# Projection steps between attention units, head-by-head turning back, and the angle steps of a rotary table in a fused two-block kernel

## The chip, the cores and the metric

One NeuronCore of a Trainium2 chip runs the whole program. The metric is the device time of one execution in microseconds (us), and of several executions the median. PE is TensorE, DVE VectorE, ACT ScalarE, POOL GpSimd, SP SyncE, whose queue issues the weight loads.

## What is computed

Two transformer blocks on one sequence of 512 tokens of 1024 channels, all in fp32. Cut to what matters here:

```
# first block (16 meta tokens in front: 528 positions)
z = rms(h) @ w_in            -> q, k, v, glu, g_att, g_conv
o = differential attention of 8 heads, block-causal mask
y_att = rms(o per head) * sub_w * 0.8
u = glu gate -> causal depthwise convolution of 31 taps -> layernorm -> silu
h = h + (sigmoid(g_att) * y_att + sigmoid(g_conv) * (u @ w_conv_out)) @ w_out
h = h + (silu(gate) * val) @ w_down      # gate, val: 3-tap conv of rms(h) @ w_up
# second block, two layers
ang = positions * inv_freq;  cos(ang), sin(ang) rotate q and k
retention of 8 heads beside a gated 3-tap convolution, one output product
```

## The kernel before, in words

Every fp32 product runs as three fp32r passes. A block of weights, 1024 x 256 (1 MB), is loaded into one of two `raw` buffers by SP's queue. ACT rounds it into `w_hi` (L965), DVE subtracts to `w_lo` (L1390, `lo(j, b)`), and PE adds up lo x hi, hi x hi, hi x lo (L414, `tile`). A **step** is one slice k of 128 input channels for one of the two output halves: three passes of two 256-column pieces, six matmuls. SP loads block b+1 into a buffer only when the `w_lo` of block b is done. Order is written out by hand on each engine, with semaphores between them.

**Attention** (PE L533 on, DVE from L1526, ACT `heads` L1045). A loop of four passes, each over two heads. A pass has ten units (`UNITS`): for each head the meta rows and then four blocks of 128 query rows. For a unit PE makes the scores (L580 to L590), DVE masks them and takes the maximum (L1557 to L1568), ACT takes the exponentials, DVE combines the two maps of the differential attention (L1573 to L1581, semaphore `a_full`), PE turns the result (`turn`, L602 and L604), ACT copies it, PE multiplies with the values (`weigh`, L619 and L621), and ACT copies that and sums its squares. Between these parts PE runs `fill(n)`, the next n of 48 projection steps (`done`, numbers 0 to 47): steps 0 to 15 the gates of this pair, 16 to 31 the q of the next, 32 to 47 the k of the next, with `jj` 0 before `jj` 1. In the fourth pass the last 32 are two blocks of the convolution's gate. The value product (`v_block`, L548) stands at the head of each pass; its first part waits for the `w_lo` that DVE made at the end of the pass before (L1612). DVE fills its own waits with taps of the 31-tap convolution (`conv`, L1474).

At the end of a pass DVE squares the exponent sums, POOL takes a power (L348), DVE scales the meta rows of both heads (`o_meta`, L1603) and then the 512 rows of one head and of the other (`o_rows`, L1609), three signals of `o_scaled`. Then it makes `lo(0, b1 + 2)`. PE's `back` (L625 to L633) waits for all three signals and transposes both heads into PSUM; DVE multiplies them by the gate (L1618, L1619) into `oT`. POOL meanwhile adds the two finished channels of the convolution to `ssum` (L371).

Behind the fourth pass DVE makes one more `w_lo` (L1621, from a `w_hi` that ACT makes when step 47 is done), PE sums `ssum` over the channels (L675), which gives the mean of the layernorm (DVE L1624), runs two gate steps and broadcasts the mean (L682), and runs 15 more gate steps while DVE and ACT centre and square.

**Feed-forward** (PE `feed_forward` L703, DVE `up` L1699 and `add_to_h` L1671): the 22 channel groups come in three parts, g = 0, g = 1 and the last. Each ends in a residual: DVE adds the product to `h` (L1678). After g = 0 DVE converts the positions to float (L1738). After g = 1 PE spreads them over the partitions (L753, one row of fp32), DVE multiplies by the frequencies (L1750, `pos_done`) and reduces the angles to the range of the sine table, seven steps for the sine and seven for the cosine (L1753 to L1760), each waiting for the one before; PE waits for `pos_done` before the last part. ACT takes the sines much later.

Of the kernel before, what the change touches and what calls it, by code (L numbers as in the profile page):

```python
# [24 lines left out]
P = 128  # L25
D = 1024
KT = D // P
SEQ = 512
META = 16
# [25 lines left out]
PI_MAX = 3.1415925  # L55
# [4 lines left out]
B_GLU, B_ATT, B_CO, B_WO, B_FF, B_LAY = 0, 4, 14, 16, 18, 35  # L60
# [3 lines left out]
FF_B = 6  # L64
# [26 lines left out]
def build(nc, io, out):  # L91
# [14 lines left out]
    with ctx:  # L106
# [10 lines left out]
        h = sb("h", [P, KT, T1])  # L117
# [279 lines left out]
        def _(pe):  # L397
# [135 lines left out]
            with pe.Fori(0, 4) as i:  # L533
# [21 lines left out]
                def fill(n):  # L555

                    for x in range(done[0], done[0] + n):
                        c, jj, k = x // (2 * KT), x // KT % 2, x % KT
                        last = tile((1, 0, 1)[c], jj, f1 + 1 + c, b1 + (c + 1) // 2, n_hi, n_lo, T1 if c == 2 else T2,
                                    part=[k], c0=0 if c == 2 else OLD)  # L560
                        if k == KT - 1:
                            last.then_inc(acc_full[jj], 1)
                    done[0] += n
# [60 lines left out]

                def back():  # L625

                    pe.wait_ge(s["o_scaled"], i * 3 + 3)
                    pe.wait_ge(s["const_done"], 4)
                    for hh in range(2):
                        for q in range(NQT):  # L630
                            pe.transpose(sc[:, hh, q * P:(q + 1) * P], o_rows[:, hh, q * P:(q + 1) * P], ident[:, :])
                        last = pe.transpose(tr[:, 0, hh * META:(hh + 1) * META], o_meta[:, hh * P:(hh + 1) * P],
                                            ident[0:META, 0:META])  # L633
                    last.then_inc(s["o_turned"], 1)
# [10 lines left out]
                fill(2)  # L645
                weigh(0)

                for uu, (n0, n1) in enumerate(((2, 2), (2, 3), (5, 1), (1, 2), (1, 1), (2, 2), (2, 2), (4, 1)), 2):
                    scores(uu)
                    fill(n0)  # L650
                    turn(uu - 1)
                    fill(n1)
                    weigh(uu - 1)
                fill(1)
                turn(UNITS - 1)
                fill(2)
                weigh(UNITS - 1)
                fill(8)
                back()
                fill(2)  # L660
                assert done[0] == 3 * 2 * KT

            def g_conv(a, b):
# [39 lines left out]
            def feed_forward(b0, f0, g0, n, kt, first=False, last=False):  # L703
                y_hi, y_lo = (g_hi, g_lo) if last else (n_hi, n_lo)

                def up_pair(i, stats=False):
                    for x, (jj, ks) in enumerate(steps_in_turn(KT)):
                        step = tile(0, jj, i * 2 + f0, i + b0, m_hi, m_lo, T2, ready=None if jj else ("n_full", KT), part=ks, c0=C2)
                        if ks[-1] == KT - 1:
                            step.then_inc(acc_full[jj], 1)  # L710
                        if stats and x == 3:
                            pe.wait_ge(s["ss_full"], 2 * KT)
                            token_sums(ST_FFN, [ssum], T2 - P)
                        if stats and x == 9:
                            broadcast(ST_FFN, [tr], T2 - SEQ)
                    chunk(1, i + b0, i * 2 + f0 + 1, m_hi, m_lo, T2, c0=C2)

                if first:
                    up_pair(0, True)
                with pe.Fori(1 if first else 0, n) as i:  # L720
                    up_pair(i)
                b, f = b0 + n, f0 + 2 * n
                for j, ks in ((0, range(kt - 2)), (1, range(3)), (0, range(kt - 2, kt)), (1, range(3, kt))):
                    for jj in range(2):
                        step = tile(j, jj, f + j, b, y_hi, y_lo, SEQ, kt, ready=("gl_full", g0) if jj == 0 else None,
                                    part=ks, bank=j, e=f + j if j == 0 else f)
                        if ks[-1] == kt - 1:
                            step.then_inc(acc_full[jj], 1)
                for j in range(1 if last else 2):
                    for jj in range(2):  # L730
                        tile(j, jj, f + 2 + j, b + 1, y_hi, y_lo, SEQ, kt, bank=j,
                             e=f + 1 + j).then_inc(acc_full[jj], 1)
                if not last:
                    return

                pe.wait_ge(lo_full[1], b + 2)
                for c in range(2):
                    for jj in range(2):
                        if c == 0:
                            pe.wait_ge(evac[jj], f + 4)  # L740
                        for k in range(kt):
                            step = half_step(1, jj, c, k, y_hi, y_lo, start=k == 0, stop=k == kt - 1)
                            if (c, jj, k) == (1, 0, 4):
                                half_sums(0, 0)
                            if (c, jj, k) == (1, 1, 4):
                                half_broadcast(ST_LAY, 0)
                        step.then_inc(s["ha_full"] if c == 0 else acc_full[jj], 1)

            for g in range(2):
                feed_forward(g * FF_B + B_FF, g * (2 * FF_B) + 2 * B_FF, g * KT, 4, KT, g == 0)  # L750

            pe.wait_ge(s["pos_f"], 1)
            pe.matmul(sc[:, 0, 0:SEQ], ones[0:1, 0:1].to_broadcast([1, P]), sin[0:1, :], start=True,  # L753
                      stop=True).then_inc(s["pos_full"], 1)
            pe.wait_ge(s["pos_done"], 1)
            feed_forward(B_FF + 2 * FF_B, 2 * (B_FF + 2 * FF_B), 2 * KT, 3, FT - 2 * KT, last=True)

# [629 lines left out]
        def _(dve):  # L1387
# [138 lines left out]
            with dve.Fori(0, 4) as i:  # L1526
# [62 lines left out]
                for hh in range(2):  # L1589
# [10 lines left out]
                                         op1=ALU.add).then_inc(s["st_var"], 1)  # L1600
                conv(2 * A_TAPS - taps[0])
                dve.wait_ge(s["st_pow"], i + ST_HEADS + 1)
                dve.tensor_tensor(o_meta[:, 0:2 * P].rearrange("p (h n) -> p h n", n=P),  # L1603
                                  o_meta[:, 0:2 * P].rearrange("p (h n) -> p h n", n=P),
                                  pw[0:META, 8:10].rearrange("p (h o) -> p h o", o=1).to_broadcast([META, 2, P]),
                                  ALU.mult).then_inc(s["o_scaled"], 1)
                for hh in range(2):
                    rows_h = o_rows[:, hh, 0:SEQ].rearrange("p (q n) -> p q n", n=P)
                    dve.tensor_tensor(rows_h, rows_h,  # L1609
                                      pw[:, 4 * hh:4 * hh + 4].rearrange("p (q o) -> p q o", o=1).to_broadcast([P, NQT, P]),  # L1610
                                      ALU.mult).then_inc(s["o_scaled"], 1)
# [115 lines left out]
                                          ALU.subtract).then_inc(s["gl_full"], 1)  # L1727
                    dve.wait_ge(s["gl_full"], tl + 2)

            for g in range(2):  # L1730
                b_g = g * FF_B + B_FF
                f_g = g * (2 * FF_B) + 2 * B_FF
                up(b_g, f_g, g * KT, 4)
                for i in range(2):
                    add_to_h(i, b_g + i + 4, f_g + i * 2 + 8)
                if g == 0:
                    dve.wait_ge(s["ld_pos"], 16)
                    dve.tensor_copy(sin[0:1, :], cos[0:1, :].bitcast(i32)).then_inc(s["pos_f"], 1)  # L1738

            dve.wait_ge(s["pos_full"], 1)  # L1740
            ang, kk = decay[:, 0, :], decay[:, 1, :]
            trig = [0]

            def t_step(ins):
                trig[0] += 1
                ins.then_inc(s["trig"], 1)
                dve.wait_ge(s["trig"], trig[0])

            dve.wait_ge(s["ld_freq"], 16)
            dve.tensor_scalar(ang, sc[:, 0, :], freq[:, 0:1], None, ALU.mult).then_inc(s["pos_done"], 1)  # L1750
            dve.wait_ge(s["pos_done"], 1)
            for dst, turn in ((sin, 0.0), (cos, 0.25)):
                t_step(dve.tensor_scalar(kk, ang, 1.0 / TWO_PI, turn, ALU.mult, ALU.add))  # L1753
                t_step(dve.tensor_scalar(kk, kk, ROUND, ROUND, ALU.add, ALU.subtract))
                t_step(dve.scalar_tensor_tensor(out=dst[:, :], in0=kk, scalar=-PI_1, in1=ang, op0=ALU.mult, op1=ALU.add))
                for part in (PI_2, PI_3):
                    t_step(dve.scalar_tensor_tensor(out=dst[:, :], in0=kk, scalar=-part, in1=dst[:, :], op0=ALU.mult,
                                                    op1=ALU.add))
                t_step(dve.tensor_scalar(dst[:, :], dst[:, :], turn * TWO_PI, PI_MAX, ALU.add, ALU.min))
                last = dve.tensor_scalar(dst[:, :], dst[:, :], -PI_MAX, None, ALU.max)  # L1760
                if dst is sin:
                    t_step(last)
            last.then_inc(s["trig_s"], 1)

            up(B_FF + 2 * FF_B, 2 * (B_FF + 2 * FF_B), 2 * KT, 3, g_hi, g_lo)
            def lo_half(jj, l):
# [283 lines left out]
```

## Time and profile before

| | |
|---|---|
| median of 3 runs | 1924.81 us (1923.0 to 1926.1) |
| the profiled execution | 1927.68 us |
| its span, first to last instruction | 1925.9 us (1.8 us lie around it) |
| PE, DVE, ACT, POOL busy | 98%, 59%, 33%, 4% |
| mean granted TensorE clock | 0.993 of full speed |
| weight load of PE busy | 88% |

Busy shares say how full an engine is, not what it waits for; a granted clock of 1.00 is 2.4 GHz and 0.50 is 1.2 GHz. The four attention passes begin at 142.54, 214.31, 286.08 and 357.83 us. The boundary behind g = 0 is at about 694 us, the one behind g = 1 at about 829 us. The duration of a matmul in the rows overlaps its neighbours'.

### The profile page before, as it was taken

To read this page: it belongs to the slowest core of one execution; us is meant where nothing else is said; L and a number is where in the kernel's file an instruction comes from. 1 tells how busy PE (TensorE), PEld (TensorE's weight loads), DVE (VectorE), ACT (ScalarE), POOL (GpSimd) and SP (SyncE) were. 2 spreads that over 40 slices of the span, in tenths; PEclk is the share of its full clock that TensorE was granted. 3 is DMA by queue.
4 is the path that set the end of the run, shared out by engine and by line. 5 is a ranking of instruction groups with operands and counts; after the bars stand their busy time and mean duration, and the time that the engine had idled before them with its cause. 6 is when DMAs were issued, how large, how long until landed. Compare 5 with 4: busy or idle time off the path is not lost.

```text
span 1925.9 us, 30697 instructions
## 1 busy us (share of the span) xinstructions
PE 1895.4 (98%) x12195; PEld 1700.1 (88%) x12195; DVE 1127.3 (59%) x1554; ACT 634.2 (33%) x1105; POOL 70.0 (4%) x72
## 2 busy tenths in 40 slices
PE   7999999999999999999999999999999999999998
PEld 7998888889999999899988888888898888888888
DVE  5777887886556546566664554454256555544522
ACT  4224454445333323224522222222242222222222
POOL 1000110110000000000000000000000000000000
PEclk8999999999999999999999999999999999999999
DMA  5221211212232223322332323233222323232231
GB/s 160 87 88 45 70 57 53 73 53 67 89 100 96 87 88 99 97 88 66 99 99 66 98 76 109 87 91 106 89 73 91 99 77 97 88 107 89 88 108 44
DMA packets 159794, 165.89 MB, mean 86 GB/s; under 512 B 3032, under 2 KB 156129, under 8 KB 159730
## 3 DMA queue, kind: packets, MB, share of 16 engines
q1 hardware_dynamic: 156736, 160.51, 25.9%
q10 hardware_dynamic: 2674, 4.42, 0.7%
q8 instruction: 46, 0.75, 0.2%
q14 instruction: 18, 0.15, 0.0%
q0 software_dynamic: 320, 0.07, 0.0%
HBM read 162.88 MB, written 2.10 MB: 86 GB/s over the span
## 4 chain that ended last, share of the span: by engine, by line
PE 89%; DVE 5%; issue 4%; ACT 1%; DMA 0%; DVEq 0%; SPq 0%; ACTq 0%; POOLq 0%; POOL 0%
PE acc L414 70%; PE acc L809 4%; PE acc L548 3%; PE acc L480 2%; PE tr L845 2%; PE acc L773 1%; PE sc L831 1%; DVE y L1474 1%; PE sc L590 1%; DVE w_lo L1390 1%; PE tr L831 1%; PE tr L621 0%; DMA xs<-in_x 0%; PE tr L619 0%; PE sc L852 0%
## 5 line engine op out<-in xcount | busy, mean ns | idle before, releaser
L1390 DVE TENSOR_TENSOR w_lo<-raw,w_hi 128x2048 fp32r<-128x2048 f32 (+1 forms) x148 | 337.6, 2281 | 151.5 <-ACT w_hi L965 150.0
L965 ACT ACTIVATE w_hi<-raw 128x2048 fp32r<-128x2048 f32 x147 | 280.0, 1905 | 433.1 <-PE acc L414 426.6
L414 PE MATMUL acc<-s_lo,w_hi 128*128 128x512 f32 x848 | 333.0, 393 | 0.0
L414 PE MATMUL acc<-s_hi,w_lo 128*128 128x512 f32 x848 | 330.2, 389 | 0.0
L414 PE MATMUL acc<-s_hi,w_hi 128*128 128x512 f32 x848 | 330.1, 389 | 0.0
L414 PE MATMUL acc<-n_lo,w_hi 128*128 128x256 f32 (+3 forms) x1024 | 240.8, 306 | 4.4 <-DVE n_lo L1424 3.0
L414 PE MATMUL acc<-n_hi,w_hi 128*128 128x256 f32 (+3 forms) x1024 | 232.1, 298 | 0.0
L414 PE MATMUL acc<-n_hi,w_lo 128*128 128x256 f32 (+3 forms) x1024 | 231.7, 297 | 0.0
L414 PEld LDWEIGHTS acc<-s_hi,w_lo 128*128 128x128 f32 x848 | 159.2, 188 | 33.3
L414 PEld LDWEIGHTS acc<-s_lo,w_hi 128*128 128x128 f32 x848 | 159.3, 188 | 32.1
L414 PEld LDWEIGHTS acc<-s_hi,w_hi 128*128 128x128 f32 x848 | 159.3, 188 | 31.9
L414 PEld LDWEIGHTS acc<-n_lo,w_hi 128*128 128x128 f32 x1024 | 163.5, 190 | 25.0 <-issue 16.8
L414 PEld LDWEIGHTS acc<-n_hi,w_lo 128*128 128x128 f32 x1024 | 164.7, 190 | 5.1
L414 PEld LDWEIGHTS acc<-n_hi,w_hi 128*128 128x128 f32 x1024 | 164.6, 190 | 4.9
L414 PE MATMUL acc<-m_hi,w_hi 128*128 128x256 f32 x832 | 166.7, 281 | 0.0
L414 PE MATMUL acc<-m_hi,w_lo 128*128 128x256 f32 x832 | 166.2, 281 | 0.0
L1474 DVE SCALAR_TENSOR_TENSOR y<-u,par,y (+1 forms) x240 | 164.5, 747 | 1.7 <-DVE neg_lam L1523 0.4
L414 PE MATMUL acc<-m_lo,w_hi 128*128 128x256 f32 x704 | 142.1, 283 | 2.2 <-DVE decay L1750 1.2
L414 PEld LDWEIGHTS acc<-m_hi,w_hi 128*128 128x128 f32 x832 | 128.2, 189 | 0.0
L414 PEld LDWEIGHTS acc<-m_hi,w_lo 128*128 128x128 f32 x832 | 127.9, 189 | 0.0
L414 PEld LDWEIGHTS acc<-m_lo,w_hi 128*128 128x128 f32 x704 | 108.2, 189 | 5.1 <-DVE z L1707 2.3
L1883 DVE SCALAR_TENSOR_TENSOR st<-sc,pp,decay 128x512 f32<-128x512 f32 (+1 forms) x32 | 20.4, 680 | 96.3 <-PE tr L831 52.1
(305 smaller groups left out, 2877.7 us busy)
## 6 DMA issues: line engine op xcount, KB each, us to landing
raw<-in_w_in SPq DMA_DIRECT2D x92, 1024.0 KB, 5.3
raw<-in_w_up SPq DMA_DIRECT2D x22, 1024.0 KB, 5.1
raw<-in_w_out SPq DMA_DIRECT2D x20, 1024.0 KB, 5.1
raw<-in_w_down SPq DMA_DIRECT2D x8, 1024.0 KB, 5.0
raw<-in_w_conv_out SPq DMA_DIRECT2D x4, 1024.0 KB, 5.1
decay<-in_decay ACTq DMA_DIRECT2D x8, 512.0 KB, 5.2
raw<-in_w_down SPq DMA_DIRECT2D x4, 768.0 KB, 4.3
xs<-in_x SPq DMA_DIRECT2D x4, 512.0 KB, 5.8
```

The lines of the kernel that those rows point to most:

```text
L414: last = pe.matmul(acc[jj][:, bank, at_:at_ + n], w[j][:, k, jj * P:(jj + 1) * P], x[:, k0 + k, c:c + n], start=start and k == 0 and p == ...
L480: last = pe.matmul(acc[jj][:, c, cols], w[j][:, k, jj * P:(jj + 1) * P], x[:, k0 + k, cols], start=start and p == 0, stop=stop and p == 2)
L548: last = pe.matmul(dst, x[:, k, c:c + m], w[0][:, k, :], start=k == 0 and p == 0, stop=k == KT - 1 and p == 2)
L590: last = pe.matmul(sc[:, m, 0:keys], qs, kT[part, hh, 0:keys], start=True, stop=True)
L773: last = pe.matmul(acc[jj][:, j, cols], w[j][:, k, jj * P:(jj + 1) * P], x[:, k, cols], start=k == 0 and w is w_hi and x is s_hi, stop=k = ...
L809: last = pe.matmul(acc[jj][:, 0, (q % 2) * CW:(q % 2 + 1) * CW], x[:, k, q * P:(q + 1) * P], w[0][:, k, :], start=k == 0 and p == 0, stop= ...
L831: last = pe.matmul(dst, rk[:, hh, kb * P:(kb + 1) * P], rq[:, hh, kb * P:SEQ], start=True, stop=True)
L845: last = pe.matmul(dst[:, q * P:(q + 1) * P], st[:, c:c + P], rv[:, kb, hh * P:(hh + 1) * P], start=kb == 0, stop=kb == q)
L965: act.activation(w_hi[j][:, 0:kt, :], raw[j][:, 0:kt, :], ACT.Copy).then_inc(hi_full[j], 1)
L1390: dve.tensor_tensor(w_lo[j][:, 0:kt, :], raw[j][:, 0:kt, :], w_hi[j][:, 0:kt, :].bitcast(fp32), ALU.subtract).then_inc(lo_full[j], 1)
L1474: dve.scalar_tensor_tensor(out=dst, in0=src, scalar=w, in1=dst, op0=ALU.mult, op1=ALU.add).then_inc(s["conv"], 1)
L1883: last = dve.scalar_tensor_tensor(out=st[:, c:c + w], in0=src, scalar=pp2[:, kb:kb + 1], in1=decay[:, hh, 0:w], op0=ALU.mult, op1=ALU.mult)
```

## The change

Three things. **Placing of steps:** one more step before `weigh(7)` (`(2, 2)` to `(2, 3)`), one more before `turn(9)`, and the two steps behind `back` are gone; the total stays 48. **Turning back head by head:** DVE scales the rows of the first head first, then the meta rows, then the rows of the second; PE's `back` transposes the first head's rows after one signal, the second's after all three, and the meta rows last. **Angles:** the spread of the positions and the sine's steps move behind the residual of g = 0, the cosine's steps behind that of g = 1; the conversion of the positions moves ahead of the residual of g = 0. PE's wait for `pos_done` stays where it was.

```diff
                 def back():
 
-                    pe.wait_ge(s["o_scaled"], i * 3 + 3)
                     pe.wait_ge(s["const_done"], 4)
                     for hh in range(2):
+                        pe.wait_ge(s["o_scaled"], i * 3 + 2 * hh + 1)
                         for q in range(NQT):
                             pe.transpose(sc[:, hh, q * P:(q + 1) * P], o_rows[:, hh, q * P:(q + 1) * P], ident[:, :])
+                    for hh in range(2):
                         last = pe.transpose(tr[:, 0, hh * META:(hh + 1) * META], o_meta[:, hh * P:(hh + 1) * P],
                                             ident[0:META, 0:META])
...
-                for uu, (n0, n1) in enumerate(((2, 2), (2, 3), (5, 1), (1, 2), (1, 1), (2, 2), (2, 2), (4, 1)), 2):
+                for uu, (n0, n1) in enumerate(((2, 2), (2, 3), (5, 1), (1, 2), (1, 1), (2, 2), (2, 3), (4, 1)), 2):
                     scores(uu)
                     fill(n0)
                     turn(uu - 1)
                     fill(n1)
                     weigh(uu - 1)
-                fill(1)
+                fill(2)
                 turn(UNITS - 1)
                 fill(2)
                 weigh(UNITS - 1)
                 fill(8)
                 back()
-                fill(2)
...
             for g in range(2):
                 feed_forward(g * FF_B + B_FF, g * (2 * FF_B) + 2 * B_FF, g * KT, 4, KT, g == 0)
-
-            pe.wait_ge(s["pos_f"], 1)
-            pe.matmul(sc[:, 0, 0:SEQ], ones[0:1, 0:1].to_broadcast([1, P]), sin[0:1, :], start=True,
-                      stop=True).then_inc(s["pos_full"], 1)
+                if g == 0:
+                    pe.wait_ge(s["pos_f"], 1)
+                    pe.matmul(sc[:, 0, 0:SEQ], ones[0:1, 0:1].to_broadcast([1, P]), sin[0:1, :], start=True,
+                              stop=True).then_inc(s["pos_full"], 1)
+
             pe.wait_ge(s["pos_done"], 1)
...
+            for g in range(2):
...
+                up(b_g, f_g, g * KT, 4)
+                if g == 0:
+                    dve.wait_ge(s["ld_pos"], 16)
+                    dve.tensor_copy(sin[0:1, :], cos[0:1, :].bitcast(i32)).then_inc(s["pos_f"], 1)
+                for i in range(2):
+                    add_to_h(i, b_g + i + 4, f_g + i * 2 + 8)
+                if g == 0:
+                    dve.wait_ge(s["pos_full"], 1)
+                    dve.wait_ge(s["ld_freq"], 16)
+                    dve.tensor_scalar(ang, sc[:, 0, :], freq[:, 0:1], None, ALU.mult).then_inc(s["pos_done"], 1)
+                    dve.wait_ge(s["pos_done"], 1)
+                    t_step(angles(sin, 0.0))
+                else:
+                    angles(cos, 0.25).then_inc(s["trig_s"], 1)
```

The seven steps themselves are those of before, put into a function `angles(dst, turn)`. On DVE the three scaling products of L1603 and L1609 are the same, in the other order.

## Rows read from the trace of the kernel before

**Rows 1.** The page, busy time by engine

```profile
PE 1895.4 (98%) x12195; PEld 1700.1 (88%) x12195; DVE 1127.3 (59%) x1554; ACT 634.2 (33%) x1105; POOL 70.0 (4%) x72
```

**Rows 2.** Waits of the PE queue, whole run: engine line waited for: us, times, longest

```profile
PE tr L602 <- DVE e L1581: 2.0, 4, 0.5
...
PE sc L590 <- ACT e L1062: 1.4, 4, 0.4
...
PE sc L631 <- DVE rb L1609: 1.1, 4, 0.3
```

**Rows 3.** Timeline of PE, second pass over a head pair: start us, us, instruction

```profile
265.57 1.13 PE L590 MATMUL sc<-kT,qT 64*128 64x512 f32 x4 [0.36 <-ACT e L1062]
...
273.43 0.28 PE L602 MATMUL tr<-ident,e 128*16 128x128 f32 x1 [0.50 <-DVE e L1581]
...
282.87 0.65 PE L631 MATMUL sc<-ident,rb 128*128 128x128 f32 x4 [0.30 <-DVE rb L1609]
```

**Rows 4.** Chain that ended last, end of that pass: start us, us, what

```profile
284.43 1.65 PE acc L414 x12
...
286.08 2.72 PE acc L548 x24
```

**Rows 5.** Timeline of DVE, same pass

```profile
267.28 0.14 DVE L1557 MEMSET sc<- 64x96 f32 x1
...
271.90 0.16 DVE L1573 TENSOR_TENSOR eu<-eu 128x2 f32<-128x2 f32 x1
...
282.74 2.27 DVE L1390 TENSOR_TENSOR w_lo<-raw,w_hi 128x2048 fp32r<-128x2048 f32 x1
...
286.27 1.40 DVE L1474 SCALAR_TENSOR_TENSOR y<-u,par,y  x2
```

**Rows 6.** Timeline of POOL, same pass, and the end of the fourth

```profile
281.55 4.64 POOL L371 TENSOR_TENSOR ssum<-ssum,y 128x514 f32<-128x514 f32 x1 [0.39 <-DVE y L1474]
286.37 2.27 POOL L371 TENSOR_TENSOR ssum<-ssum,y 128x514 f32<-128x514 f32 x1 [0.18 <-POOL ssum L371]
...
429.86 1.10 POOL L371 TENSOR_TENSOR ssum<-ssum,y 128x514 f32<-128x514 f32 x1 [0.18 <-POOL ssum L371]
```

**Rows 7.** Timeline of PE behind the fourth pass

```profile
431.10 1.25 PE L675 MATMUL sc<-ones,ssum 128*128 128x1 f32 x10 [1.50 <-POOL ssum L371]
...
434.55 2.29 PE L682 MATMUL tr<-ident,var 128*128 128x128 f32 x10 [0.32 <-DVE var L1624]
```

**Rows 8.** Timeline of ACT behind the fourth pass

```profile
429.69 0.60 ACT L974 ACTIVATE ga<-acc 128x514 f32<-128x514 f32 x1 [6.61 <-PE acc L414]
430.19 1.90 ACT L965 ACTIVATE w_hi<-raw 128x2048 fp32r<-128x2048 f32 x1
```

**Rows 9.** Windows: stretch us, busy us by engine, PEclk, DMA share, GB/s

```profile
432.00:440.00 8.00, 7.68 (x41) 7.38 (x41) 5.20 (x7) 1.99 (x5) 0.00 (x0) 0.58 0.52 177
832.00:840.00 8.00, 8.00 (x57) 8.00 (x57) 7.62 (x13) 0.00 (x0) 0.00 (x0) 0.79 0.01 2
```

**Rows 10.** Chain that ended last, both group boundaries of the second feed-forward part

```profile
717.47 22.19 PE acc L414 x186
...
831.40 24.42 PE acc L414 x192
```

**Rows 11.** Timeline of PE at the second group boundary

```profile
829.06 1.12 PE L753 MATMUL sc<-sin,ones 1*128 1x512 f32 x2
831.40 0.47 PE L414 MATMUL acc<-m_lo,w_hi 128*128 128x256 f32 x2 [1.23 <-DVE decay L1750]
```

**Rows 12.** Timeline of DVE behind the first and the second group boundary

```profile
703.30 0.69 DVE L1707 TENSOR_TENSOR z<-acc,rb 128x514 f32<-128x514 f32 x1 [5.23 <-PE acc L414]
...
830.22 0.75 DVE L1750 TENSOR_SCALAR decay<-sc,freq 128x512 f32<-128x512 f32 x1 [0.36 <-PE sc L753]
...
838.93 2.28 DVE L1390 TENSOR_TENSOR w_lo<-raw,w_hi 128x2048 fp32r<-128x2048 f32 x1
```

**Rows 13.** The page, DMA issues: out<-in, queue, times, KB each, us to landing

```profile
raw<-in_w_up SPq DMA_DIRECT2D x22, 1024.0 KB, 5.1
```

More of the change, by code:

```diff
@@ L1602, in _ @@
                 dve.wait_ge(s["st_pow"], i + ST_HEADS + 1)
[L1603 to L1606, printed above, removed]
                 for hh in range(2):
+                    if hh == 1:
+                        dve.tensor_tensor(o_meta[:, 0:2 * P].rearrange("p (h n) -> p h n", n=P),
+                                          o_meta[:, 0:2 * P].rearrange("p (h n) -> p h n", n=P),
+                                          pw[0:META, 8:10].rearrange("p (h o) -> p h o", o=1).to_broadcast([META, 2, P]),
+                                          ALU.mult).then_inc(s["o_scaled"], 1)
                     rows_h = o_rows[:, hh, 0:SEQ].rearrange("p (q n) -> p q n", n=P)
@@ L1728, in up @@
                     dve.wait_ge(s["gl_full"], tl + 2)
[L1730 to L1740, printed above, removed]
             ang, kk = decay[:, 0, :], decay[:, 1, :]
@@ L1747, in t_step, with angles @@
                 dve.wait_ge(s["trig"], trig[0])
[L1749 to L1752, printed above, removed]
+            def angles(dst, turn):
                 t_step(dve.tensor_scalar(kk, ang, 1.0 / TWO_PI, turn, ALU.mult, ALU.add))
@@ L1759, in _ @@
                 t_step(dve.tensor_scalar(dst[:, :], dst[:, :], turn * TWO_PI, PI_MAX, ALU.add, ALU.min))
[L1760 to L1763, printed above, removed]
+                return dve.tensor_scalar(dst[:, :], dst[:, :], -PI_MAX, None, ALU.max)
+            for g in range(2):
+                b_g = g * FF_B + B_FF
+                f_g = g * (2 * FF_B) + 2 * B_FF
+                up(b_g, f_g, g * KT, 4)
[12 more added lines that the diff above has]
+                    angles(cos, 0.25).then_inc(s["trig_s"], 1)
             up(B_FF + 2 * FF_B, 2 * (B_FF + 2 * FF_B), 2 * KT, 3, g_hi, g_lo)
```

## The prediction

> **What bounds the kernel now.** I read the page's busy times first: PE is busy 98% of the span [rows 1], so only PE's idle time and its low clock can be won. PE's waits come next. In each of the four attention passes PE waits three times for something that this change touches: for the exponentials in front of the last scores, for DVE in front of the last `turn`, for DVE's scaled rows in front of `back`, four times each, 4.5 us in all [rows 2]. The timeline of the second pass shows the three, 0.36, 0.50 and 0.30 us [rows 3]. The other places are the way out of attention, with 1.50 and 0.32 us of idling [rows 7], and the second group boundary, with 1.23 us [rows 11]. Behind each of these two the granted clock was 0.50, that is 1.2 GHz, for some time [rows 9]. The range that the changed kernel can move in is therefore small: I take 0.2% (3.9 us) as what a measurement can tell from no change.
>
> **Steps and turning back, passes one to three.** A step of six matmuls lasts 22.19 / 186 x 6 = 0.72 us [rows 10]. The added step before `weigh(7)` brings PE to the last scores 0.72 later, where 0.36 was idle: they start 0.36 later. DVE's next mask begins at 267.28 and the scores end near 266.7, so 0.36 fits there [rows 3, 5]. But the scores hold back `fill(4)` and `turn(8)`; ACT copies that turn before it takes the second half of the last unit's exponentials, and DVE starts on those at 271.90, just when they come [rows 5]. I take 0.3 us of delay for DVE from here on (bounds 0 and 0.36). PE was ready for `turn(9)` at 272.93; with 0.36 and another step it is ready at 274.0, DVE's result at 273.8: no wait, and PE is 0.58 later than before. `back` is reached at 282.57 + 0.58 = 283.15; the first head's rows are ready at 282.5 and the second's at 283.1, before PE needs either. So the new order of turning back covers nothing once the steps have moved: with one wait for all three signals PE would stand within 0.1 us of where it does. It costs nothing either: ten transposes stay ten.
>
> `back` took 284.43 - 282.87 = 1.56 [rows 3, 4]; it now ends at 284.7. Before, two steps (1.65) stood behind it and the value product began at 286.08 [rows 4]. They are gone, and the value product waits for `w_lo`, which DVE ends at 282.74 + 2.27 = 285.01 [rows 5], now 285.3. That wait was hidden under the two steps; it becomes visible with 0.6 us. With 0.1 for a start that is not overlapped, a pass ends at 285.45 in place of 286.08: 0.6 us won, not 1.16. Bounds: 0.5 (DVE 0.36 late, slower restart) and 0.9 (DVE not late). Three passes: -1.8 (-1.5 to -2.7).
>
> **The way out of attention.** The fourth pass is the second moved by 429.86 - 286.37 = 143.49 us [rows 6]. `back` ends near 428.2 in its frame. PE then needs POOL's sum. Before, POOL ended it at 430.96 and PE had two steps to run; now it has none and idles from 428.2. DVE's taps are 0.3 late, so the sum is too, were it alone. It isn't. Step 47 ends before `back` instead of behind it, so ACT, idle for 6.61 us until then, makes the last `w_hi` some 3 us earlier [rows 8], and DVE goes from `oT` into that `w_lo` without a gap. POOL's second addition is then beside a DVE product with two SBUF inputs. The rows have the price: the same addition took 1.10 us where DVE was idle and 2.27 where two taps (1.40 us) ran beside it, and 4.64 for the first one, beside the row scaling, `w_lo` and `oT` [rows 5, 6]. POOL does about its 1.1 us of work once DVE is through. With 2.27 us of `w_lo` in front, the sum ends near 433.4 instead of 430.96: +2.4. Bounds: +0.3 (not blocked) and +3.5 (it shares badly and loses all of 4.64).
>
> That leaves PE idle for 5.4 us where it had 1.50, and the clock, which fell a little after the shorter gap [rows 9], is down already when PE resumes. Then `ssum`'s ten narrow matmuls, two steps at 1.2 GHz (2.6 for 2.0: in the window from 832 a mean of 0.79 over 8 us is 3.4 us at 0.50, and 1.51 us were lost in them, so work runs at 0.55 of its pace [rows 9, 10]), and the broadcast, slow before as well. The 0.32 us wait for the mean goes, since `w_lo` is done sooner [rows 7]. So the broadcast starts 2.4 + 0.1 + 0.6 - 0.3 = 2.8 us later in the pass's frame. A mean of 0.58 over the 8 us from 432 is 6.7 us at 0.50 [rows 9], some 3 of them behind the broadcast; I add 0.2 for a longer stay (bounds 0 and 1.6). The way out costs +3.0 (bounds +0.1 and +4.5).
>
> **Angles.** At the second boundary PE ran the spread, 1.1 us, idled 1.23 and then ran 192 matmuls in 24.42 us [rows 10, 11]. At the usual pace these take 22.19 x 192 / 186 = 22.91: 1.51 us went to the low clock, seen in the window from 832 [rows 9]. Removed: 1.1 + 1.2 + 1.5 = 3.8, less 0.1 for the wait for DVE's residual that the others hide: -3.7. The spread itself goes to the first boundary, +1.1 less 0.1. There PE goes on at once, since `pos_done` is asked for one part later; without a gap behind it I expect no fall of the clock (bounds 0 and +1.5, the price at the old place). DVE gets the multiplication and the sine's steps at the first boundary: half of 838.93 - 830.22, some 4.7 us [rows 12]. It was idle for 5.23 us ahead of the next `z` [rows 12], and that `z` comes 1.1 later: covered with 1.6 to spare; without cover PE would wait the rest for its accumulators. The cosine's 4.0 at the second boundary fit the same way. The block behind this `w_lo` is asked for 4 us later on SP's queue and lands in 5.1 [rows 13], long before it is due one 22.19-us chunk later. The conversion moved ahead of the residual lies in DVE's idle time. Together -2.7 (-1.2 to -2.9).
>
> **Sum.** -1.8 + 3.0 - 2.7 = -1.5 us against the profiled execution's 1927.68: 1926.2. That execution is 2.87 above the median, so the median goes from 1924.81 to 1923.3.
>
> **A rule beside it.** The rows say that POOL's addition waits for DVE's products from SBUF. The Trainium skill, SBUF — State Buffer, in "Who interferes with whom", says that a DVE instruction with two SBUF inputs and a GpSimd instruction that reads SBUF exclude each other for a whole instruction, and that the one issued first has its way. By that rule the order decides, which is the second rival below.
>
> **Rivals.**
> - *Forecast (0.52):* POOL blocked, `w_lo` visible at the head of passes two to four, angles won: 1921.5 to 1925.5.
> - *POOL first (0.25).* If POOL takes up the second addition ahead of DVE's `w_lo`, the sum is 0.3 late, not 2.4, and DVE's delay of 1.1 falls on nothing, because that `w_lo` isn't read in the 16 gate steps that come next, and the mean's scaling behind it is still no later than before. The way out then costs 0.3 + 0.1 + 0.6 - 0.3 = 0.7: -1.8 + 0.7 - 2.7 = -3.8, 1921.0. Against it: behind the same `oT` DVE's taps began at 286.27 and POOL's addition at 286.37, and the taps won [rows 5, 6]. For it: 0.10 us is little.
> - *Little hidden at the pass heads (0.10).* If DVE isn't late and PE's three waits all go with `w_lo` in time, a pass gives 1.16, which with POOL blocked is -1.7 more than forecast: 1921.6; with POOL first, 1919.3. Against it: DVE is without a gap from the last mask to `w_lo`, 285.01.
> - *The clock, on the slower side (0.13).* The place is PE's idle stretch behind the fourth pass and the spread at the first boundary. If the narrow spread lets the clock fall there as at its old place, the angles give 1.2, and if the clock behind the longer gap stays low to the end of its worse bound, the way out costs 4.5: -1.8 + 4.5 - 1.2 = +1.5, 1926.3. It decides the sign once the low clock costs over 1.5 us beyond what the forecast gives it. For it: both gaps in the old trace were followed by 1.2 GHz. Against it at the boundary: it has no gap there.
>
> **Numbers.** Likeliest 1923.3. The range takes in POOL first and most of the clock case: 1920.3 to 1926.5. Faster by over 0.2% (below 1921.0) needs POOL first or free pass heads with luck: 0.22. Slower by over 0.2% (above 1928.7) needs more than the clock case: 0.04. Within 0.2%: 0.74.
>
> **What would show it.** Right: PE's waits for `e`, and for `rb` at `back`, gone; a new wait for `w_lo` of 0.5 to 0.8 us in front of the value product, three times; passes of about 71.2 us; POOL's eighth addition over 3 us and PE waiting more than 4 us for it; no wait for `decay`, and the second boundary's chunk in 22.9 us. Wrong: POOL's eighth addition still 1.1 us; passes of 70.6; a low clock behind 694 us; a DVE wait at the first boundary that PE feels.

## The result, and the profile after

Slower. Of 9 executions each, taken in turn on one chip, the changed kernel has a median of 1930.17 us (1927.12 to 1932.14) and the kernel before one of 1924.27 us (1923.0 to 1927.8). The ratio is 1.0027, 95% interval 1.0018 to 1.0036: +5.9 us by the medians, where the prediction had -1.5 and a range that ended at 1926.5. The profiled execution of the changed kernel is its slowest, 1932.14 us (span 1930.0), beside 1927.68 of the kernel before: +4.46 between the two traces. It is also the one with the lowest mean granted clock of the nine, 0.990; the other eight have 0.991 to 0.994.

The page of the changed kernel, busy time by engine and the waits of the PE queue (engine, line, what for: us, times, longest), beside [rows 1, 2]:

```profile
PE 1896.5 (98%) x12195; PEld 1703.1 (88%) x12195; DVE 1131.4 (59%) x1554; ACT 634.9 (33%) x1105; POOL 64.9 (3%) x72
```

```profile
PE acc L548 <- DVE w_lo L1391: 4.2, 3, 1.4
PE sc L631 <- DVE rb L1611: 3.6, 4, 0.9
...
PE sc L675 <- DVE oT L1621: 2.7, 1, 2.7
```

PE's busy time hardly moved and its number of matmuls not at all, so nothing was computed more. Two of the three old waits, for the exponentials and for DVE in front of the last `turn`, are gone, and so are the waits at the second group boundary. But the wait in front of turning back, 0.3 each time in [rows 2, 3], is now 0.9, and the value product waits 1.4 us for `w_lo` three times, where I had said 0.6. DVE is 4 us busier and POOL 5 us less: a hint already that the two stand in each other's way elsewhere than before.

The end of the second pass, DVE's timeline (start us, us, instruction), beside [rows 5]:

```profile
284.18 0.68 DVE L1611 TENSOR_TENSOR rb<-rb,pw 128x512 f32<-128x512 f32 x1
284.78 1.51 DVE L1606 TENSOR_TENSOR sq<-sq,pw 16x256 f32<-16x256 f32 x1
286.22 0.67 DVE L1611 TENSOR_TENSOR rb<-rb,pw 128x512 f32<-128x512 f32 x1
286.82 2.27 DVE L1391 TENSOR_TENSOR w_lo<-raw,w_hi 128x2048 fp32r<-128x2048 f32 x1
```

POOL's, beside [rows 6], with the end of the fourth pass:

```profile
284.52 1.49 POOL L371 TENSOR_TENSOR ssum<-ssum,y 128x514 f32<-128x514 f32 x1 [0.39 <-DVE y L1475]
286.19 3.86 POOL L371 TENSOR_TENSOR ssum<-ssum,y 128x514 f32<-128x514 f32 x1 [0.18 <-POOL ssum L371]
...
432.29 1.49 POOL L371 TENSOR_TENSOR ssum<-ssum,y 128x514 f32<-128x514 f32 x1 [0.39 <-DVE y L1475]
433.96 3.86 POOL L371 TENSOR_TENSOR ssum<-ssum,y 128x514 f32<-128x514 f32 x1 [0.18 <-POOL ssum L371]
```

And PE's, beside [rows 3, 4]:

```profile
285.45 0.60 PE L631 MATMUL sc<-ident,rb 128*128 128x128 f32 x4
286.95 0.66 PE L631 MATMUL sc<-ident,rb 128*128 128x128 f32 x4 [0.90 <-DVE rb L1611]
287.53 0.29 PE L633 MATMUL tr<-ident,sq 16*128 16x16 f32 x2
289.22 0.57 PE L548 MATMUL acc<-w_hi,n_lo 128*128 128x256 f32 x1 [1.40 <-DVE w_lo L1391]
289.60 0.41 PE L548 MATMUL acc<-w_hi,n_hi 128*128 128x256 f32 x1
```

Read the three together. The scaling of the meta rows, 16 partitions by 256, takes 1.51 us, where the kernel before has 0.40 for the same work. And POOL's first addition, which took 4.64 us beside three DVE products (two row products and `w_lo`) in [rows 6], is through in 1.49. POOL asked at 284.52, in the course of the first row product, was served when that ended at about 284.9, and held the meta product until 286.0. DVE is 1.1 us later from there, and with it everything behind it in its queue: the second head's rows (PE idle 0.90) and `w_lo` (PE idle 1.40). Then comes a second price. The matmuls of L548 follow each other in 0.21 us where 0.11 is their pace at the full clock. The windows (stretch us, busy us by engine, PEclk, DMA share, GB/s) and the chain of the changed kernel say why:

```profile
288.00:296.00 8.00, 6.78 (x37) 6.48 (x38) 4.20 (x9) 0.38 (x4) 2.05 (x1) 0.57 0.42 131
360.00:368.00 8.00, 5.70 (x50) 5.01 (x48) 6.94 (x10) 2.41 (x2) 5.07 (x2) 1.00 0.31 100
432.00:440.00 8.00, 4.46 (x32) 3.95 (x31) 8.00 (x10) 2.40 (x2) 5.34 (x2) 0.92 0.21 68
440.00:448.00 8.00, 8.00 (x47) 8.00 (x48) 3.23 (x7) 1.90 (x4) 0.00 (x0) 0.66 0.61 195
```

```profile
213.98 5.48 PE acc L548 x24
...
289.22 5.48 PE acc L548 x24
...
295.42 5.66 PE acc L548 x48
...
364.42 3.10 PE acc L548 x24
...
367.99 5.66 PE acc L548 x48
```

At the head of the third pass the mean granted clock is 0.57, and the 24 matmuls of the value product's first part take 5.48 us for the 2.72 of [rows 4], at the head of the second and the third pass. At the head of the fourth, behind the same two gaps, they take 3.10 at a granted 1.00. So the clock falls there in some passes and not in others. From this part to the next it is 6.20 us with the low clock and 3.57 without: the fall costs 2.6 us. (The 3.10 is 0.4 more than [rows 4] have, at the full clock too; that belongs to the section on the prediction.)

Where the 4.46 us between the two traces are, by the starts of the value products (before 142.38, 214.15, 285.92, 357.67; after 141.62, 213.98, 289.22, 364.42) and of L675 (before 431.10, after 438.25): ahead of attention -0.76; pass one +0.59, pass two +3.47, pass three +3.45, which is +7.5; the way out to L675 73.83 for 73.43, +0.4, and +0.2 from there to the 570 matmuls of the last projection (488.11 before, 495.46 after); from there to the last instruction -3.2, of which the two group boundaries have -2.8 (+0.9 and -3.7); and +0.4 outside the span. The second and third pass have 2.6 us of low clock each in them.

### The profile page after: what moved, and what is told of

The parts are those of the page before. It is cut to its first block, busy times and chain, and to the rows that moved or that the text cites. A ratio compares the mean times of both kernels' runs of the same rounds, so it can differ in the third digit from the quotient of the medians.

```text
span 1930.0 us, 30698 instructions
## 1 busy us (share of the span) xinstructions
PE 1896.5 (98%) x12195; PEld 1703.1 (88%) x12195; DVE 1131.4 (59%) x1554; ACT 634.9 (33%) x1105; POOL 64.9 (3%) x72
## 4 chain that ended last, share of the span: by engine, by line
PE 91%; DVE 4%; issue 2%; ACT 1%; DMA 0%; DVEq 0%; SPq 0%; ACTq 0%; POOLq 0%; POOL 0%
PE acc L414 72%; PE acc L810 4%; PE acc L548 3%; PE acc L480 2%; PE tr L846 2%; PE acc L774 1%; PE sc L832 1%; PE sc L590 1%; DVE y L1475 1%; DVE w_lo L1391 1%; PE tr L621 1%; PE tr L832 1%; PE tr L619 0%; DMA xs<-in_x 0%; PE tr L604 0%
```

## The experiments

All are compared with the kernel before on the same chip in the same rounds; its medians were 1924.34 (e1 to e4, 33 executions), 1925.76 (e5 to e8, 15) and 1924.53 (e9 to e11, 27), on three different chips. So a time of one group is set against a time of another with each one's own kernel before taken off. The ratios lie nearer to those of the means than of the medians (e3: 3.15 us by the medians, 2.05 by the means, 1.0010 in the table).

**The parts alone.** e2 is the kernel before with the placing only, e3 with the scaling order and the turning back only, e4 with the angles only; e1 is the changed kernel with one thing undone, the place of the meta product:

```diff
 # e1: the changed kernel, DVE's three products in the order meta, rows 0, rows 1
-                        pe.wait_ge(s["o_scaled"], i * 3 + 2 * hh + 1)
+                        pe.wait_ge(s["o_scaled"], i * 3 + hh + 2)
...
 # e2: the kernel before, and
+   (2, 3) for the seventh pair, fill(2) ahead of turn(UNITS - 1)
-   fill(2) behind back()
 # e3: the kernel before, and back() and the order of L1603/L1609 as in the change
 # e4: the kernel before, and the moves of the angles as in the change
```

The expectations say "port theory" for this: the cost comes from POOL's first addition getting between DVE's products, since the two wait for each other.

> The changed kernel with one thing undone: DVE scales the meta rows first again, then the rows of head 0, then of head 1; PE still turns back head by head. Port theory: in the changed kernel POOL's first addition gets in between the row product and the short meta product, DVE stands 1.1 us in each pass, w_lo is 1.4 us late at the pass heads and the clock falls there. Then here POOL's first addition is over 4 us again, the meta product 0.4 us, PE waits 0.3 to 0.7 us for w_lo three times, no 1.2 GHz at the pass heads, and the time is 1922 to 1926 us. Placing theory (the two steps that stood behind the turning back are what is missing, whatever DVE does first): low clock at the pass heads stays, 1928 to 1931 us.

> The kernel before with the placing of the steps alone; scaling order, turning back and angles as before. Port theory: passes of about 71.2 us, no fall of the clock at the pass heads, way out of attention 1 to 4 us dearer; 1924 to 1928 us, which is e1 plus 2.7 for the angles. Placing theory: the whole loss and the angles' 2.7 missing: 1931 to 1934 us.

> The kernel before with the scaling order and the head-by-head turning back alone; the two steps stay behind it. Port theory: meta product 1.5 us, POOL's first addition 1.5 us, rows of head 1 and w_lo 1.1 us late; PE waits about 1 us inside the turning back in place of 0.3, w_lo stays hidden under the two steps: passes 0.4 to 0.8 us longer, POOL's sum sooner at the way out; 1923 to 1928 us. Placing theory: nothing but what the trace of before had, 1924 within 1 us, meta product 0.4 us.

> The kernel before with the angle steps and the spread of the positions moved, attention as before. Both theories: the wait for pos_done and the low clock behind 829 us gone, spread 1.1 us at the first boundary without a fall of the clock: 2.7 us faster, 1921 to 1922.5 us. If the spread costs a low clock at its new place: 1923 us.

| | median us | executions | ratio, 95% interval | passes 1 to 3, us |
|---|---|---|---|---|
| e1 meta product first | 1926.01 | 11 | 1.0006 [0.9997, 1.0015] | 71.3, 71.4, 71.5 |
| e2 placing only | 1927.5 | 11 | 1.0014 [1.0005, 1.0023] | 71.3, 71.5, 71.5 |
| e3 turning back only | 1927.49 | 11 | 1.0010 [1.0001, 1.0019] | 72.2, 72.3, 72.3 |
| e4 angles only | 1923.44 | 11 | 0.9990 [0.9981, 0.9999] | as before |

e1 to e3 come out at the upper ends of the ranges of the port theory (e1 at 1926.01 for 1926). e4's median is 0.9 us above its range, its profiled execution (1921.28) inside of it. e3 shows the POOL addition by itself. Its waits of PE, and POOL and DVE in its second pass:

```profile
PE sc L631 <- DVE rb L1611: 3.8, 4, 1.0
```

```profile
281.32 1.48 POOL L371 TENSOR_TENSOR ssum<-ssum,y 128x514 f32<-128x514 f32 x1 [0.39 <-DVE y L1475]
```

```profile
280.98 0.68 DVE L1611 TENSOR_TENSOR rb<-rb,pw 128x512 f32<-128x512 f32 x1
281.58 1.50 DVE L1606 TENSOR_TENSOR sq<-sq,pw 16x256 f32<-16x256 f32 x1
```

With all the projection steps where they were, the new order alone makes the meta product 1.50 us long and PE's wait 1.0, and a pass 0.5 longer; the two steps behind `back` still hide `w_lo`, and the clock doesn't fall. e1 keeps everything of the change but that order, and its waits and POOL's second pass read:

```profile
PE sc L675 <- POOL ssum L371: 5.9, 1, 5.9
...
PE acc L548 <- DVE w_lo L1391: 4.2, 3, 1.4
```

```profile
280.93 4.62 POOL L371 TENSOR_TENSOR ssum<-ssum,y 128x514 f32<-128x514 f32 x1 [0.40 <-DVE y L1475]
...
428.58 3.17 POOL L371 TENSOR_TENSOR ssum<-ssum,y 128x514 f32<-128x514 f32 x1 [0.18 <-POOL ssum L371]
```

POOL is shut out again (4.62), passes are 71.3 to 71.5, and the granted clock is 1.00 at the head of each. That is 4.2 us under the changed kernel by the medians, and the interval of its ratio ends (1.0015) below that of the change (from 1.0018). PE's wait for `w_lo` is 1.4 us, though, where I had expected 0.3 to 0.7. The same trace has the cost that I had forecast for the way out: the eighth addition takes 3.17 us beside the last `w_lo`, and PE waits 5.9 for it. e2 has both, too (3.17; 5.2). By the means of the executions, each against the kernel before in its own rounds, the parts give +2.3, +2.1 and -2.2, together +2.2, and the change +5.5: the first two make more together than one by one. What each lacks alone is the other half of a gap. e2 waits 0.7 us for `w_lo`, e3 1.0 for the rows, e1 1.4 for `w_lo`, and the clock stays up; the changed kernel has 0.9 and then, 0.9 us of transposes later, 1.4, and it falls.

**What lets POOL in.** Two theories about the meta product: that its few partitions matter (e5 makes it as wide as the others), or its place between two row products (e6 puts it last).

```diff
 # e5: the changed kernel; the scaled buffer has unused rows behind the meta rows
-                        dve.tensor_tensor(o_meta[:, 0:2 * P]..., o_meta[:, 0:2 * P]..., pw[0:META, 8:10]...
+                        dve.tensor_tensor(sq[:, 0, 0:2 * P]..., sq[:, 0, 0:2 * P]..., pw[:, 8:10]...
 # e6: the changed kernel; DVE scales rows 0, rows 1, meta; PE's second wait is for all three
```

> The changed kernel, order kept (rows of head 0, meta, rows of head 1), but the meta product is taken over all 128 partitions (128x256 in place of 16x256; the 112 other rows are scratch). Asks why POOL's addition gets in just there. If it is the change from 128 to 16 partitions that lets it in: meta product 0.4 us, POOL's first addition over 4 us, 1925 to 1927 us as in e1. If any other product between the two of one loop lets it in (another tile, another place in the queue): 1.5 us for the meta product as in the changed kernel, 1929 to 1931 us.

> The changed kernel with the meta product behind both row products. If the change of partitions lets POOL in: POOL's first addition starts to count behind the second row product, meta product 1.5 us, rows of head 1 on time, w_lo 1.1 us late, POOL's first addition about 2.1 us, 1928 to 1931 us. If it is the middle place that matters: POOL's first addition over 4 us, 1925 to 1927 us.

e5: 1936.74 us (4 executions), ratio 1.0057 [1.0041, 1.0072]. e6: 1935.4 us (4), 1.0048 [1.0033, 1.0064]. Both are worse than the change and slower than either branch that I had set for them, since in both POOL gets in twice. PE then waits 1.8 us for the scaled products and 1.4 for `w_lo`, and the low clock follows at three of the three pass heads in e5 and at two in e6 (the 24 matmuls in 5.48, 5.24, 4.62 and 5.48, 3.09, 4.38 us). POOL and DVE in e5, then POOL and DVE in e6, second pass:

```profile
286.20 1.49 POOL L371 TENSOR_TENSOR ssum<-ssum,y 128x514 f32<-128x514 f32 x1 [0.39 <-DVE y L1475]
287.87 1.10 POOL L371 TENSOR_TENSOR ssum<-ssum,y 128x514 f32<-128x514 f32 x1 [0.18 <-POOL ssum L371]
```

```profile
287.89 1.62 DVE L1611 TENSOR_TENSOR rb<-rb,pw 128x512 f32<-128x512 f32 x1
```

```profile
286.36 1.48 POOL L371 TENSOR_TENSOR ssum<-ssum,y 128x514 f32<-128x514 f32 x1 [0.39 <-DVE y L1475]
288.02 1.33 POOL L371 TENSOR_TENSOR ssum<-ssum,y 128x514 f32<-128x514 f32 x1 [0.18 <-POOL ssum L371]
```

```profile
286.01 2.38 DVE L1606 TENSOR_TENSOR rb<-rb,pw 128x512 f32<-128x512 f32 x2
288.31 1.31 DVE L1609 TENSOR_TENSOR sq<-sq,pw 16x256 f32<-16x256 f32 x1
```

Neither the width nor the middle place is the condition. What the two share with the changed kernel and e3 is what DVE does when POOL asks. Both start from the same event, the end of POOL's power: DVE's first product begins at once, POOL's addition 0.35 us later. If the first product is the meta one (0.34 us long), that is the moment at which the row product starts, and POOL is shut out; if it is a row product (0.6), POOL asks in its middle and is served at its end.

**POOL made to ask at another moment.** e9 and e10 leave DVE's and PE's order as the change has it and only add a wait on POOL:

```diff
                 pool.wait_ge(s["conv"], i * (2 * A_TAPS) + (8 * G_TAPS + 2 * A_TAPS))
+                pool.wait_ge(s["o_scaled"], i * 3 + 3)      # e9;  i * 3 + 1 in e10
```

> The changed kernel, with one wait more on POOL: its first addition of a pass asks only when all three scaling products are done, so it can't get in between them. If POOL's addition inside the scaling is what makes the change slow: the meta product is back to 0.41 us, the scaling products follow each other without a gap, PE's waits for rb fall from 0.9 to under 0.3 each, w_lo ends some 1.1 us sooner, the clock doesn't fall at the pass heads, passes of 71.5 to 71.9 us, and the whole near 1926 (ratio 1.000 to 1.001), as when the meta product stood first. If the order of turning back or the late DVE alone is the cause: passes stay at 75 us and the whole at 1930.

> The changed kernel, with POOL's first addition released by the first scaling product: it asks within 0.2 us of the meta product's start, not 0.34 us into the product of the first head's rows. If a request gets in because it arrives while a full-width product runs with another product behind it: it now stands in the course of the short meta product, waits or gets in ahead of the second head's rows; getting in there delays PE's second wait and w_lo by 1.1 us again, 1929 to 1931. If a request that arrives within 0.1 us of a product's start is shut out until DVE's row of products ends: no delay, POOL's addition ends behind w_lo as before (over 3.5 us long), near 1926.

e9: 1926.49 us (11 executions), 1.0007 [0.9998, 1.0016]. e10: 1925.69 us (10), 1.0003 [0.9994, 1.0013]. One added wait undoes 3.9 to 4.7 us by the medians, and both intervals end below that of the change. POOL in e9, then e10's POOL and DVE, second pass:

```profile
282.92 3.10 POOL L372 TENSOR_TENSOR ssum<-ssum,y 128x514 f32<-128x514 f32 x1 [1.92 <-DVE rb L1612]
```

```profile
281.76 4.02 POOL L372 TENSOR_TENSOR ssum<-ssum,y 128x514 f32<-128x514 f32 x1 [0.99 <-DVE rb L1612]
```

```profile
280.82 0.68 DVE L1612 TENSOR_TENSOR rb<-rb,pw 128x512 f32<-128x512 f32 x1
281.42 0.41 DVE L1607 TENSOR_TENSOR sq<-sq,pw 16x256 f32<-16x256 f32 x1
281.76 0.67 DVE L1612 TENSOR_TENSOR rb<-rb,pw 128x512 f32<-128x512 f32 x1
282.36 2.27 DVE L1392 TENSOR_TENSOR w_lo<-raw,w_hi 128x2048 fp32r<-128x2048 f32 x1
```

In e10 the release reached POOL later than the 0.2 us I had written: it asked at 281.76, just as the second row product began, and it waited for that and for `w_lo` and ended 1.2 us behind `w_lo`. The second branch of the expectation held, and so did the first one of e9. In both kernels the meta product is back to 0.41, PE waits 1.4 us for `w_lo` three times, not for the rows, and the clock is 1.00 at the pass heads, with passes of 71.3 to 71.5. So the place of the meta product costs nothing by itself; that POOL gets in costs.

**The way out and DVE's length.** e7 is e1 with the last `w_lo` behind the mean's scaling on DVE. e8 is e7 with four of the seven taps that DVE runs behind the last mask moved to the second unit, where it waits for PE.

```diff
 # e7
-            lo(1, B_CO - 1)
             dve.wait_ge(s["mean_sum"], 1)
...
+            lo(1, B_CO - 1)
             start_sum(1)
 # e8, besides
-                    conv((3, 2, 3, 3, 4)[uu % 5])
+                    conv((3, 2, 3, 3, 4)[uu % 5] + (4 if uu == 1 else 0))
...
-                conv(7)
+                conv(3)
 # e11: e4 (angles only), and the two conv lines of e8
```

> e1 (1926.0 us) with the last w_lo of the way out moved behind the scaling of the mean on DVE. Blocking theory: POOL's eighth addition takes 3.17 us in e1 since that w_lo stands beside it; here 1.1 us, PE's wait for the sum 3.8 in place of 5.9 us, and 2 to 3 us less in all: 1923 to 1924.5 us. If POOL is slow for another reason the wait stays at 5.9 and the time at 1926.

> e7 with four taps of the convolution taken from behind the last unit of a pass to the second unit, where DVE idles over 5 us. DVE theory (DVE's chain from the last mask to w_lo sets the pass, the steps moved by the change are only worth what DVE leaves): DVE some 1.4 us earlier, waits for w_lo at the pass heads 0 to 0.3 us, passes 70.6 to 70.9 us in place of 71.45, POOL's sum 1.4 us earlier, 1918.5 to 1921.5 us. If PE's own work sets the pass: passes stay at 71.4 and only the way out gains, 1922 to 1924 us.

> The kernel before with the angle steps moved and four of the convolution's taps moved from behind the last mask to the second unit, projection steps and turning back as before. If the four taps gain by themselves (DVE earlier everywhere at the end of a pass): some 6 us under the kernel before with the angles alone, 1917 to 1919. If DVE's earlier w_lo is worth something only where the two steps behind turning back are gone: what is won are the old waits for e and rb, at most 0.8 us in each pass, so 1920 to 1923, and the moved steps are worth 3 us or more once DVE is early.

| | median us | executions | ratio, 95% interval | passes, us | PE waits: `w_lo`; POOL's sum |
|---|---|---|---|---|---|
| e7 | 1924.24 | 11 | 0.9989 [0.9980, 0.9998] | 71.3, 71.5, 71.5 | 1.4 x3; 3.8 |
| e8 | 1917.52 | 5 | 0.9959 [0.9945, 0.9972] | 69.9, 70.1, 70.1 | none; 2.5 |
| e11 | 1920.18 | 11 | 0.9977 [0.9968, 0.9986] | 71.3, 71.3, 71.3 | none; 0.6 |

POOL's eighth addition in e7:

```profile
429.38 1.09 POOL L371 TENSOR_TENSOR ssum<-ssum,y 128x514 f32<-128x514 f32 x1 [0.18 <-POOL ssum L371]
```

Without a `w_lo` beside it the addition takes 1.09 us for 3.17, and the wait for it falls by 2.1, as the expectation of e7 had it: that term had the right mechanism and nearly the size (2.27). e8's DVE and its chain, end of the second pass:

```profile
279.43 2.27 DVE L1391 TENSOR_TENSOR w_lo<-raw,w_hi 128x2048 fp32r<-128x2048 f32 x1
```

```profile
280.67 0.87 PE sc L631 x8
281.55 0.22 PE tr L633 x2
281.77 0.07 issue
281.84 3.10 PE acc L548 x24
```

`w_lo` ends at 281.70, just ahead of the value product at 281.84, and a pass takes 70.1 us. Against e11's 71.3 this is the 1.1 and more that the placing and the new turning back can give, once DVE isn't what a pass ends on: e8 is 6.7 us under e7, and 1 us under the range that I had set (its passes were to be 70.6 to 70.9). It beats both kernels, the one before by 8.2 us by the medians. e11 tells how much of that is the taps alone: with the old steps and the old turning back they give 3.5 us (against e4). The moved steps, the new turning back and e7's `w_lo` give the rest: 2.7 by the medians of e11 and e8 as they stand, 3.9 with each one's own kernel before taken off; the three passes alone are 3.6 shorter. The lower end of my second branch, 1920, is where it came out, though not for its reason: the waits for `e` are all still there (2.0 and 1.4 us in four), and of the three only the one for the rows is gone; a pass is 0.5 shorter.

## Why the prediction was wrong, point by point

- **The step that failed: "the new order of turning back covers nothing [...] It costs nothing either: ten transposes stay ten."** I costed it by PE's instructions alone. Its cost was on DVE's queue: the order of three products there decides what DVE is doing 0.35 us after POOL's power, and with a row product first POOL's addition gets between. That is 1.1 us in each pass (1.51 for 0.41), shown by e3, e1, e9 and e10. The row that I used for another term, 4.64 us for an addition that began beside the row products [rows 6], said that POOL was being kept out; the question that I didn't ask of it is what the new order does to that.
- **The clock at the pass heads.** No rival had it; my clock case stood behind the fourth pass and at the first boundary. With 0.9 and 1.4 us of idling close together the granted clock fell at two of three pass heads of the profiled execution, 2.6 us each. It comes with the failed step: with POOL held back (e1, e9, e10) 1.4 us alone left it at 1.00. No trace shows where it falls in other executions, but each has its mean granted clock: in the changed kernel 0.990 in the profiled one, 0.992 in the middle, 0.994 in the shortest (1927.12 us) and in one of 1930.09 us, and 0.993 or 0.994 in all of e1. So the trace has more of it than is usual. From e1 to the changed kernel it is 3.3 us of POOL in three passes, less 2.4 that the way out gains (133.41 to 131.04, below), and 4.2 in all by the medians: an estimate of some 3 us of clock in a usual execution.
- **Passes one to three without POOL, -1.8.** Direction right, size too large: e1 gives -0.5, -0.4 and -0.3 us (71.3, 71.4, 71.5 for 71.77), -1.2. DVE was late by 0.4 for 0.3 (in e1 it idles 0.32 for the last exponentials, as reckoned). PE was ready 0.4 sooner than I had it: with the meta rows together at the end, `back` takes 1.26 us for 1.56 (281.86 to 283.12). It bought nothing. Two things were mis-sized besides. The 0.6 us were the distance from 285.45 to 286.08, and the second is a start by the chain; PE's timeline, by which passes are measured here, has 285.92, so the forecast was worth 0.47. And I gave 0.1 us to a value product that starts behind the transposes. Its first part takes 2.99 to 3.10 us for 2.72 at the heads of passes two to four in e1, at a granted 1.00, and 3.10 in e8, where it doesn't wait; why is open. From the last mask on DVE sets the end of a pass, and PE's gains there turned into a wait for `w_lo` of 1.4 for my 0.6.
- **The way out, +3.0.** Right for the kernel that I had in mind, and not for the one that ran. In e1 the blocked addition took 3.17 us and PE waited 5.9 (I said more than 4), and from the fourth value product to the 570 matmuls of the last projection it took 133.41 us for 130.44: +3.0, at a granted 0.57 from 432 to 440. In the changed kernel POOL was through at 437.82, ahead of the last `w_lo` at 438.12, since its first addition had got in, and the same stretch took 131.04, +0.6. What was lost in front was in part regained here, by another road than the rival "POOL first", whose price for this part was right (0.7) and whose contest, with the last `w_lo`, didn't take place.
- **Angles, -2.7.** Right in the trace. At the two boundaries the changed kernel is 2.8 us shorter, 3.7 less at the second and 0.9 more at the first, with no fall of the clock behind the spread there:

```profile
700.99 1.12 PE L753 MATMUL sc<-sin,ones 1*128 1x512 f32 x2
```

```profile
702.11 22.83 PE acc L414 x192
...
838.15 22.19 PE acc L414 x186
```

192 matmuls in 22.83 us is the usual pace (22.91 by [rows 10]). e4 alone gives less outside the trace, -2.2 by the means and -0.9 by the medians. DVE had 2.29 us to spare ahead of the next `z`, for my 1.6.
- **From one trace to the median.** I took the profiled execution's 2.87 us above the median for a constant and subtracted it. The kernel before lies anywhere from 1923 to 1928 us on one chip, and its trace is one of the long ones, with a low clock at both of the places in [rows 9]; e4's profiled execution, 1921.28 us, has none behind the fourth pass. e4's mean granted clocks fall into two groups: 0.995 or 0.996 in five executions of 1921.28 to 1922.64 us, 0.994 in six of 1923.44 to 1924.27. A third place varies that no edit touches: the 18 matmuls of L480 from 934.64 take 3.57 us before, with a mean granted clock of 0.84 from 936 to 944, and 2.25 in e4 at 1.00; nine of the thirteen traces have a low clock there, e2, e4, e8 and e11 have none. If shorter executions have a fall less, part of the 1.5 us that I let the angles win isn't in the median to be won. That fits e4, and e1, whose trace is 1.8 us shorter in span than the one of before and whose mean is 0.9 longer. It isn't shown for the angles' own term: there is one trace of each.
- **Rivals.** None of the four came out. The slower side was looked for at the way out, where the longest gap was; a mechanism that repeats three times in the loop would have been the one to price.
- **The rule beside it.** The Trainium skill, SBUF — State Buffer, "Who interferes with whom", has the two engines exclude each other for a whole instruction and the first issued win. The traces agree with the first half: no DVE product was cut into, and POOL in the middle of one waited for its end. With the second half they differ: POOL's addition asked at 281.55 [rows 6], and the second row product and `w_lo`, which started at about 282.1 and at 282.74 [rows 5], still went ahead of it. By that rule read on every pair of products, the order of DVE's three would have had to be looked at; I weighed it for the eighth addition only.

## What to carry to other kernels

Where two engines shut each other out, as DVE's products and POOL's additions do here, reordering instructions of equal cost isn't free: ask what the one is doing at the moment at which the other asks, and if it gets in, who is queued behind. A load-bearing row like "4.64 us for 1.1 us of work" is a state that a reordering can flip; one semaphore wait that pins the request's moment (e9, e10) makes it safe. And before work is taken away from behind a wait, look whose end the wait really is: here the placing and the new turning back paid 1.1 us a pass only after DVE's row was shortened (e8 against e11).

## What the runs showed of the hardware that I had not expected

- **Who goes first when DVE has products queued.** POOL asking 0.33 to 0.35 us into a product was served at that product's end, before the next one, in every trace (changed kernel, e3, e5 and e6, with a second time in e6). In e9 it was served at the end of `w_lo`, where DVE's next products, `oT` with one input in PSUM, ran beside it in their usual 0.67 us. POOL asking within 0.1 us of a product's start waited for all of the queued ones (before, e1, e2, e10, and the second addition of the changed kernel: 3.86 us), with one exception, the second addition of e5 (asked at 287.87, product at 287.89, served at once, while e3's second, asked at 282.99 with the product at 283.01, waited). Why so long a queue goes ahead of it, and why e5 differs, stays open; no run varied the moment in finer steps.
- **The clock.** PE gaps of 0.9 and 1.4 us with 0.9 us of work between were followed by 1.2 GHz at two of three pass heads, for 5.5 us and more, and gaps of 1.8 and 1.4 us at five of six (e5, e6); a single gap of 1.4 us at the same place (e1, e7, e9, e10) was not. Behind the fourth pass e1's 5.9 us were followed by it, and in e4's profiled execution the old gap of about 1.5 us was not, though it was in the kernel before [rows 9]: e4's trace is flattered by that.
- Ten transposes took 0.3 us less when the two narrow ones stood together at the end than between the wide ones (1.56 in [rows 3, 4], 1.26 in e1; by the chains 1.34 in e11 and 1.09 in e8, neither of which waits in front of them).
